# Gate map of the experts: gates split in a high and a low part, six of eight gated one-hots from GpSimd

## The reference, cut to what matters

```python
# per token: 128 choices = 8 heads x 16; expert = 128 * i + j, a gate for each
act = gelu(einsum('tkd,td->tk', u_emb[eb], tb), approximate=False) * gb
return einsum('tk,tkd->td', act, v_emb[eb])
```

## Time and profile before

| what | value |
|---|---|
| median of 3 runs | 2372.04 us (2369.4 to 2373.62) |
| the profiled execution, its own time | 2367.97 us |
| its span in the trace | 2366.1 us |
| steps with a group of one-hots, about | 1680 to 1917 us of the span |
| steps without | 1917 to 1995 us |
| granted TensorE clock, both stretches | 1.00 of full speed |
| PE busy over the span | 2271.9 us (96%) |
| DVE busy | 1615.5 us (68%) |
| ACT busy | 1040.3 us (44%) |
| POOL busy | 110.4 us (5%) |

### The profile page before, as it was taken

How to read it: one execution, slowest core, us unless ns; L and a number is a source line. 1 busy time by engine, 2 the same in 40 slices (tenths; PEclk the granted TensorE clock), 3 DMA queues, 4 the chain that set the end, 5 groups by cost and what they waited for, 6 DMA issues and landing times. The chain is left out here.

```text
span 2366.1 us, 46054 instructions
## 1 busy us (share of the span) xinstructions
PE 2271.9 (96%) x18286; PEld 2132.5 (90%) x18286; DVE 1615.5 (68%) x3000; ACT 1040.3 (44%) x1688; POOL 110.4 (5%) x42
## 2 busy tenths in 40 slices
PE   7999999999999998999799998989999999999997
PEld 7999789999999887999789997989999998888886
DVE  5665567664765466766476667689889975777775
ACT  5443455443544345544363435434444444333333
POOL 0000000000000000000000000069300000000000
PEclk9999999999999999999898998999999999999999
DMA  5563434554455342456332225535444445555553
GB/s 192 171 200 118 169 109 135 177 193 147 143 174 197 122 145 81 152 187 205 113 129 73 82 82 172 167 118 169 142 141 138 142 161 169 188 194 192 191 194 133
DMA packets 99245, 361.12 MB, mean 153 GB/s; under 512 B 11496, under 2 KB 15224, under 8 KB 98944
## 3 DMA queue, kind: packets, MB, share of 16 engines
q1 hardware_dynamic: 99072, 358.64, 45.8%
HBM read 357.55 MB, written 1.05 MB: 152 GB/s over the span
## 5 line engine op out<-in xcount | busy, mean ns | idle before, releaser
L876 DVE TENSOR_TENSOR w_lo<-ring,w_hi 128x1024 fp32r<-128x1024 f32 (+1 forms) x304 | 397.6, 1308 | 241.3 <-ACT w_hi L693 241.0
L693 ACT ACTIVATE w_hi<-ring 128x1024 fp32r<-128x1024 f32 (+1 forms) x304 | 341.3, 1125 | 401.8 <-PE ps L427 364.2
L427 PE MATMUL ps<-x_hi,w_hi 128*128 128x272 f32 (+1 forms) x1664 | 488.2, 293 | 18.0 <-DVE w_lo L876 16.5
L427 PE MATMUL ps<-x_hi,w_lo 128*128 128x272 f32 (+1 forms) x1664 | 479.1, 288 | 0.0
L427 PE MATMUL ps<-x_lo,w_hi 128*128 128x272 f32 (+1 forms) x1664 | 478.4, 288 | 0.0
L427 PEld LDWEIGHTS ps<-x_hi,w_hi 128*128 128x128 f32 x1664 | 314.5, 189 | 25.2 <-issue 10.7
L427 PEld LDWEIGHTS ps<-x_lo,w_hi 128*128 128x128 f32 x1664 | 314.1, 189 | 1.0
L427 PEld LDWEIGHTS ps<-x_hi,w_lo 128*128 128x128 f32 x1664 | 314.5, 189 | 0.0
L234 ACT ACTIVATE v_gated_hi<-ring 128x1024 fp32r<-128x1024 f32 x128 | 135.9, 1062 | 214.7 <-PE ps L2863 214.0
L2650 PE MATMUL ps<-tok_hi,u_mid_hi 128*128 128x256 f32 x736 | 213.6, 290 | 1.3 <-POOL u_mid_lo L240 1.3
L2650 PE MATMUL ps<-tok_hi,u_mid_lo 128*128 128x256 f32 x736 | 208.1, 283 | 0.0
(11 more groups left out here) (479 smaller groups left out, 5029.8 us busy)
## 6 DMA issues: line engine op xcount, KB each, us to landing
ring<-in_gate_up SPq DMA_DIRECT2D x176, 512.0 KB, 3.3
ring<-in_peer_v SPq DMA_DIRECT2D x128, 512.0 KB, 3.2
ring<-in_peer_u_mid SPq DMA_DIRECT2D x92, 512.0 KB, 3.3
ring<-in_down SPq DMA_DIRECT2D x64, 704.0 KB, 4.1
ring<-in_w_in SPq DMA_DIRECT2D x46, 512.0 KB, 3.3
ring<-in_peer_u_early SPq DMA_DIRECT2D x36, 512.0 KB, 3.2
ring<-in_project SPq DMA_DIRECT2D x32, 512.0 KB, 4.1
ring<-in_na_qk SPq DMA_DIRECT2D x16, 512.0 KB, 3.8
```

The source lines that it names most:

```text
L427: mm = nc.tensor.matmul(ps[:, bank, 0:ntok], parts[left][:, slot, t * P:(t + 1) * P], rhs[right][:, k, 0:ntok], start=start and n == 0, st ...
L693: A.activation(parts[0][:, n % SLOTS, 0:width[n]], ring[:, n % SLOTS, 0:width[n]], ACT.Copy).then_inc(hi_done.sem, 1)
L876: V.tensor_tensor(parts[1][:, n % SLOTS, 0:width[n]], ring[:, n % SLOTS, 0:width[n]], parts[0][:, n % SLOTS, 0:width[n]].bitcast(F32), ALU ...
```

## The change

The gate is split in a high part (rounded to fp32r by an ACT copy) and a low part (a DVE subtraction), as all other operands of the kernel are, so that the product of one token becomes two fp32r matmuls with the same `hot_j` (hi, then lo) that add up in PSUM. `gated_i` becomes two tiles, `gated_i_hi` and `gated_i_lo`; a group of four tokens now needs eight gated one-hots. Two (hi of tokens 0 and 1) stay on DVE, six move to GpSimd, in this order: hi of tokens 2 and 3, lo of tokens 0 to 3. PE waits for both engines. `hot_j` stays on DVE, with fp32r as its type. The gate parts and `late_gelu` lie in columns 1024 to 1279 of the ring's slots, which this stage's loads don't touch.

```diff
-        hot_j = sb_in(build, "hot_j", [P, 2, 4, P])
-        gated_i = sb_in(build, "gated_i", [P, 2, 4, P])
-        late_gelu = sb_in(build, "late_gelu", [P, 2, SEQ])
+        hot_j = sb_in(build, "hot_j", [P, 2, 4, P], F32R)
+        gated_i = [sb_in(build, f"gated_i_{part}", [P, 2, 4, P], F32R) for part in ("hi", "lo")]
+
+        gate_parts = [ring[:, part, D:D + SEQ] for part in range(2)]
+        late_gelu = ring[:, 2:4, D:D + SEQ]
...
+        DVE_HOTS = ((0, 0), (0, 1))
+        POOL_HOTS = ((0, 2), (0, 3), (1, 0), (1, 1), (1, 2), (1, 3))
...
                     pe.wait_ge(hots.sem, g + 1)
+                    pe.wait_ge(pool_hots.sem, g + 1)
...
                     for n in range(4):
-                        mm = nc.tensor.matmul(ps[:, g % 2, P * n:P * n + P], gated_i[:, g % 2, n, :], hot_j[:, g % 2, n, :], start=True, stop=True)
+                        for part in range(2):
+                            mm = nc.tensor.matmul(ps[:, g % 2, P * n:P * n + P], gated_i[part][:, g % 2, n, :], hot_j[:, g % 2, n, :],
+                                                  start=(part == 0), stop=(part == 1))
...
+                pool.wait_ge(loaded.sem, loaded.at(16))
+                pool.wait_ge(gate_lo_done.sem, 1)
+                for g in range(TG):
+                    if g >= 2:
+                        pool.wait_ge(spread.sem, g - 1)
+                    for part, n in POOL_HOTS:
+                        t = 4 * g + n
+                        last = nc.gpsimd.tensor_scalar(gated_i[part][:, g % 2, n, :], iota[:, :], sel_t[:, 0, t:t + 1], gate_parts[part][:, t:t + 1],
+                                                       ALU.is_equal, ALU.mult)
+                    last.then_inc(pool_hots.sem, 1)
...
+                act.wait_ge(sel_copied.sem, 1)
+                A.activation(gate_parts[0].bitcast(F32R), sel_t[:, 2, :], ACT.Copy).then_inc(gate_hi_done.sem, 1)
...
-                    for n in range(4):
+                    for part, n in DVE_HOTS:
                         t = 4 * g + n
-                        V.tensor_scalar(gated_i[:, b, n, :], iota[:, :], sel_t[:, 0, t:t + 1], sel_t[:, 2, t:t + 1], ALU.is_equal, ALU.mult)
+                        V.tensor_scalar(gated_i[part][:, b, n, :], iota[:, :], sel_t[:, 0, t:t + 1], gate_parts[part][:, t:t + 1], ALU.is_equal, ALU.mult)
...
-                dve.wait_ge(sel_copied.sem, 1)
+                dve.wait_ge(gate_hi_done.sem, 1)
+                V.tensor_tensor(gate_parts[1], sel_t[:, 2, :], gate_parts[0], ALU.subtract).then_inc(gate_lo_done.sem, 1)
```

More of the change, by code:

```diff
@@ L2601, in peer @@
         iota = sb_in(build, "iota", [P, P])
-        hot_j = sb_in(build, "hot_j", [P, 2, 4, P])
-        gated_i = sb_in(build, "gated_i", [P, 2, 4, P])
-        late_gelu = sb_in(build, "late_gelu", [P, 2, SEQ])
+        hot_j = sb_in(build, "hot_j", [P, 2, 4, P], F32R)
+        gated_i = [sb_in(build, f"gated_i_{part}", [P, 2, 4, P], F32R) for part in ("hi", "lo")]
+        gate_parts = [ring[:, part, D:D + SEQ] for part in range(2)]
+        late_gelu = ring[:, 2:4, D:D + SEQ]
         iota4 = iota[:, :].unsqueeze(1).broadcast_to([P, 4, P])
         w, wm = W["peer_u_early"], W["peer_u_mid"]
+        gate_hi_done, gate_lo_done, pool_hots = flags("gate_hi_done", "gate_lo_done", "pool_hots")
         (scored, score_kept, picked, exp_in, exp_out, sel_turned, sel_copied, mid_done, mid_gelu, mid_taken, hots, spread,
```

## The result

| | before | changed |
|---|---|---|
| median | 2370.88 us (4 runs, 2369.4 to 2373.62) | 2515.4 us (4 runs, 2511.22 to 2516.0) |
| ratio | | 1.0604, 95% interval 1.0586 to 1.0623 |
| span of the profiled execution | 2366.1 us | 2514.2 us |

The change costs 6%, 144.5 us by the medians and 148.1 us between the two traces. It lies outside the range of the prediction, on the side that was forecast. The windows of the changed kernel answer to the earlier trace rows: two stretches with one-hots, one without.

What follows compares the result with a forecast made beforehand. PE was taken to bound the kernel at 3.76 us per step; POOL and DVE in turns make it 1.77 + 6 x 0.47 = 4.59 us, 52 us over 63 steps, plus 2 once: 2425 us, range 2366 to 2505.

Steps and rivals of the forecast that it cites:

- What bounds before: Steps with one-hots in the kernel before: PE is busy throughout and sets the 3.76 us step.
- PE's term: Products on PE: eight records per group at 0.112 us each, nothing gained and nothing lost.
- the row with 64 moving columns: Earlier trace's PE record: 128-column stationary tiles with 64 moving columns start 0.112 us apart, taken as load-bound.
- The rival with 0.065 us: Products on PE cost 0.065 us and POOL keeps up: 23 us saved, about 2348 us; chance 0.12.
- the one with four passes: Rival on PE: fp32r products need full float32 passes, 0.224 us each, 57 us more, 2429 us; chance 0.05.
- POOL's price: Time of one gated one-hot on POOL: taken as 0.47 us, six per group 2.8 us.
- the nearer bounds: Limits for one POOL one-hot: 0.29 us by columns alone, 0.65 us by POOL against DVE at the low part.
- "much slower" rival: POOL's one-hots cost over 0.65 us or turns cost more; with 0.8 us, 2550 us; chance 0.10.
- What comes on top: POOL and DVE exclude each other in SBUF, so their times add: 1.77 us per step, upper bound 2.44.
- Once: Start of the stage: the first group waits for ACT, DVE and six POOL one-hots, 2 us.
- The range: Total time: from 2366 us (same time less noise) to 2505 us (a POOL one-hot of 0.65 us, some dearer turns).
- t = 0.65: POOL one-hot time t in us used for the upper end: a 5.67 us step, 120 us more plus 2.

Runs made afterwards that it cites:

- e3: Changed kernel with only the four hi one-hots, on DVE, and the hi part multiplied twice; 2372.32 us, 1.0007 of the kernel before.
- e4: Changed kernel with only the four hi one-hots, on DVE, the hi part multiplied once in two halves of 64 columns; 2371.08 us, 1.0005 of before.
- e9: Changed kernel without GpSimd one-hots: DVE makes the four hi ones, ACT the lo ones as scaled copies; 2377.59 us, 1.0044 of before.
- e7: Changed kernel with GpSimd's one-hots only 16 columns wide from group 2 on; 2410.24 us, 1.0177 of before.
- e6: Changed kernel with two constants in place of the pointer scalars in GpSimd's six one-hots; 2485.72 us, 1.0493 of before.
- e11: Changed kernel plus one unused DVE instruction of 512 columns per group with two SBUF inputs; 2547.3 us, 1.0748 of before.
- e12: Changed kernel plus one unused DVE MAX8 per group over 512 columns of one SBUF input; 2515.76 us, 1.0617 of before.

## Why the prediction missed

**What bounds before, and PE's term: right.** Products of 128 columns cost 0.112 us, as the row with 64 moving columns said, so eight of them are the 0.89 us of before; e3, e4 and e9 show it three ways. The rival with 0.065 us and the one with four passes are both refuted. The Trainium skill, "TensorE: Matmul & The Clock Gate", gives 81 ns for short matmuls in its section on the back-to-back issue gap, which would have been wrong here; its load rule (section LDWEIGHTS, 107 ns for 128 columns) was near the 112 measured.

**POOL's price: the step that failed.** "I take the middle, 0.47 us" stood between 0.29 (by columns) and 0.65 us (by DVE's one-hot and the ratio of the low parts). Measured is 0.775 us, above the upper of the nearer bounds. e7 shows what the price is made of: a column costs 3.4 ns and not 2.3, and some 0.34 us are fixed, where the column bound had no fixed part and the ratio of a two-input instruction was carried over to another kind. Why GpSimd needs this much stays open; e6 leaves only 0.07 us of it to the pointers. The term enters six times: 6 x (0.775 - 0.47) = 1.8 us of a step, 115 us of 63. My "much slower" rival had this price (0.8 us) with a chance of 0.10, and gave 2550 us.

**What comes on top: right in kind, its size too large.** I forecast 1.77 us of turns per step; measured are 1.3 us. e11 and e12 show that it is in the main DVE's two-input reads. The forecast that the low part would take over 1.23 us in many records came true for 19 of 64. What was wrong is "an instruction waits for the other's whole instruction": DVE waited 0.2 us at most for a one-hot of 0.79, where a DVE instruction under a POOL low part waited nearly its full 2.42 us, and two thirds of DVE's low parts didn't wait at all. The two errors of size together: predicted 1.77 + 2.82 = 4.59, measured 1.3 + 4.65 = 5.95 us. With the measured price alone, the forecast's sum would have been 1.77 + 4.65 = 6.42 us per step, about 2540 us.

**Once: too small.** I gave 2 us; PE stood 7.3 us in front of the first group, since POOL's first two one-hots, which overlap with DVE's `hot_j` of two groups and two low parts, took 4.9 us together:

```profile
1680.59 4.94 POOL L2694 TENSOR_SCALAR gated_i_hi<-iota,sel_t,ring 128x128 fp32r<-128x128 f32 x2 [3.49 <-DVE ring L2832]
1685.51 3.11 POOL L2694 TENSOR_SCALAR gated_i_lo<-iota,sel_t,ring 128x128 fp32r<-128x128 f32 x4
```

**The sum as it was.** Between first and last product 375.3 us against 238.4 (1678.8 to 1917.2) are 136.9 us; 7.3 us of the first wait; 2.5 us by which this execution was late before the change's first instruction (`sel_t` at 1678.60 in its timeline, 1676.10 in the earlier trace rows); together 146.7 of the 148.1 between the spans. The lower clock (0.86) should cost nothing of its own, as POOL sets the pace and has no idle time; no run parts the two.

**The range.** Its upper end took t = 0.65, the bound by ratio, as nearly the worst. An operation that no row shows on its engine can lie outside bounds that are made from another operation or another engine.

## What to carry to other kernels

Before work is moved to an engine that has no row of it, measure one instruction of that kind: a price that enters six times per step decides more than the whole of the rest. On GpSimd many small instructions are the dear form (here an estimated 0.34 us each before the first column), and much of what DVE reads through two SBUF inputs is added on top.

The product of one token was two matmuls with a weight load each as full float32, and as two fp32r parts it still is; with a moving side of 128 columns each costs 0.112 us either way, and nothing is won. A type whose tile loads faster won here: bfloat16 halved the product (0.056 us), with the loss of precision that it brings, and then DVE is level with PE.

## What the runs showed of the hardware that was not expected

- GpSimd's `TENSOR_SCALAR` of 128 fp32 columns with two pointer scalars: 0.775 us from start to start; 0.705 with constants; 0.39 with 16 columns. DVE's takes 0.256. The Trainium skill, "GPSIMD Engine Reference", section Engine selection, calls one-input operations roughly line-rate; these rows don't bear that out at this size.
- Contention was uneven: POOL's short instructions were stretched from 0.79 to as much as 1.9 us under DVE's (2.6 in the first group), while DVE's low parts took 1257 ns on average against 1225, and 1434 at most. The Trainium skill, "SBUF — State Buffer", section Who interferes with whom, says that whoever issues first gets the pair of ports for the whole instruction and the other fully blocks. That fits the long POOL instructions of the earlier trace rows and DVE's side here. It doesn't fit POOL's one-hots: a low part that began 0.08 to 0.27 us into one got in at some 0.29 us, and one that began later didn't wait, though the one-hot lasted 0.79.
- A load of a 128-column tile took 192 ns in fp32r and 98 ns in bfloat16, and the products with it 0.112 and 0.056 us. The Trainium skill, "TensorE: Matmul & The Clock Gate", section on the weight-path perf modes, says that fast weight load is on for inputs other than FP32; the runs agree if fp32r counts as FP32, whose load took 192 ns too.
